# Attention on one Trainium2 core: exponentials turned unnormalised into alternating banks, values per branch in one pass, query tiles in order 3 0 2 1

## The reference

```python
p_c = _masked_softmax(s_c, (cmp_end[None, :] <= t[:, None]))     # compressed keys, 31 of them
o_c = jnp.einsum('bgrqn,bngd->bqgrd', p_c, v_cmp)
...
s_s = s_s - slopes[...] * d_s                                     # keys of the same sequence
p_s = _masked_softmax(s_s, m_s)
o_s = jnp.einsum('bgrqm,bgqmd->bqgrd', p_s, v_sel)
...
p_w = _masked_softmax(s_w, m_w)                                   # window of 512 keys
o_w = jnp.einsum('bgrqk,bkgd->bqgrd', p_w, vwb)
return gate0 * o_c + gate1 * o_s + gate2 * o_w                    # then * silu(z), then @ w_out
```

## Time and profile before

| what | value |
|---|---|
| median of 3 runs | 1343.09 us (1340.88 to 1346.35) |
| the profiled execution, its own time | 1339.4 us |
| its span in the profile | 1337.6 us |
| PE busy | 1275.8 us, 95% |
| DVE, ACT, POOL busy | 788.0 us, 434.3 us, 840.3 us |
| granted clock of PE, mean | 0.991 |
| attention stage, first scores to first matmul of the output product | 852.83 to 1017.81 us |

### The profile page before, as it was taken

How to read it: one execution, slowest core, us unless ns; L and a number is a source line. 1 busy time by engine, 2 the same in 40 slices (tenths; PEclk the granted TensorE clock), 3 DMA queues, 4 the chain that set the end, 5 groups by cost and what they waited for, 6 DMA issues and landing times.

```text
span 1337.6 us, 22823 instructions
## 1 busy us (share of the span) xinstructions
PE 1275.8 (95%) x8112; PEld 1015.6 (76%) x8112; DVE 788.0 (59%) x1214; ACT 434.3 (32%) x866; POOL 840.3 (63%) x1062
## 2 busy tenths in 40 slices
PE   6999998999999999999999999899999999999996
PEld 4778897778877788888788798555557787878884
DVE  5978664589699211598347235378773649832223
ACT  4165744243301133211200021677773200331111
POOL 6767632677999777899678728200003875467872
PEclk9999999899999999999999999999999999999998
DMA  5222100253325433354494213100004469623331
GB/s 194 74 85 79 49 4 16 79 140 94 95 78 198 158 101 94 93 159 150 110 349 133 73 30 95 32 2 1 1 1 160 147 143 265 207 72 97 100 95 71
DMA packets 86478, 137.93 MB, mean 103 GB/s; under 512 B 16512, under 2 KB 34432, under 8 KB 85376
## 3 DMA queue, kind: packets, MB, share of 16 engines
q1 hardware_dynamic: 48384, 88.10, 22.1%
q10 hardware_dynamic: 38016, 48.71, 11.5%
HBM read 119.02 MB, written 20.91 MB: 105 GB/s over the span
## 4 chain that ended last, share of the span: by engine, by line
PE 81%; DVE 8%; issue 4%; POOL 3%; ACT 2%; ACTq 1%; DMA 1%; POOLq 0%; DVEq 0%
PE ps L388 20%; PE ps L389 20%; PE ps L390 20%; PE ps L783 3%; PE ps L794 3%; PE ps L806 3%; PE ps L541 2%; POOL small L1404 2%; DVE acc L1494 1%; PE ps L687 1%; PE ps L732 1%; DVE bigB L1991 1%; PE ps L862 1%; POOL wh L1405 1%; PE ps L531 1%
## 5 line engine op out<-in xcount | busy, mean ns | idle before, releaser
L1407 POOL TENSOR_TENSOR wl<-raw,wh 128x512 fp32r<-128x512 f32 x336 | 500.4, 1489 | 27.0
L1404 POOL TENSOR_TENSOR small<-small 1x1 f32<-1x1 f32 x336 | 122.0, 363 | 304.4 <-PE ps L390 298.2
L388 PE MATMUL ps<-uH,wh 128*128 128x512 f32 x672 | 266.6, 397 | 11.1 <-DVE uL L1484 11.1
L390 PE MATMUL ps<-uH,wl 128*128 128x512 f32 x672 | 263.0, 391 | 0.0
L389 PE MATMUL ps<-uL,wh 128*128 128x512 f32 x672 | 262.7, 391 | 0.0
L1405 POOL CAST wh<-raw 128x512 fp32r<-128x512 f32 x336 | 202.9, 604 | 0.0
L388 PEld LDWEIGHTS ps<-uH,wh 128*128 128x128 f32 x672 | 127.0, 189 | 40.6 <-issue 11.2
L389 PEld LDWEIGHTS ps<-uL,wh 128*128 128x128 f32 x672 | 127.1, 189 | 27.3 <-issue 1.4
L390 PEld LDWEIGHTS ps<-uH,wl 128*128 128x128 f32 x672 | 126.9, 189 | 26.6
L388 PE MATMUL ps<-ffH,wh 128*128 128x512 f32 x256 | 101.3, 396 | 4.4 <-POOL wl L1407 4.3
L389 PE MATMUL ps<-ffL,wh 128*128 128x512 f32 x256 | 99.8, 390 | 0.0
(11 more groups left out here) (387 smaller groups left out, 2428.2 us busy)
## 6 DMA issues: line engine op xcount, KB each, us to landing
raw<-wstream SPq DMA_DIRECT2D x336, 256.0 KB, 2.6
b_powers_scratch<-bigB ACTq DMA_DIRECT2D x4, 1024.0 KB, 4.9
c_powers_scratch<-bigB ACTq DMA_DIRECT2D x8, 512.0 KB, 4.4
lags_scratch<-lag_rows_scratch ACTq DMA_DIRECT2D x8, 512.0 KB, 9.0
bigB<-b_powers_scratch ACTq DMA_DIRECT2D x4, 1024.0 KB, 8.9
bigB<-lags_scratch ACTq DMA_DIRECT2D x4, 1024.0 KB, 5.9
bigB<-c_powers_scratch ACTq DMA_DIRECT2D x4, 1024.0 KB, 9.0
hT<-x ACTq DMA_DIRECT2D x4, 512.0 KB, 7.3
```

What stands on the lines that cost most here:

```text
L388: pe.matmul(out, lh, rh, start=first, stop=False)
L390: return pe.matmul(out, ll, rh, start=False, stop=last)
L1404: pool.tensor_tensor(small[0:1, 569 + j:570 + j], zero_ap[0:1], zero_ap[0:1], ALU.add)
L1407: pool.tensor_tensor(wl[:, j, :], raw[:, j, :], wh[:, j, :].bitcast(f32), ALU.subtract).then_inc(half_split, 1)
```

## The change

- **Units** become (t, b, qt) with qt in the order 3, 0, 2, 1: four units make a *group*, one head pair and one branch; there are 16 groups.
- **`weigh` is gone.** `prob` (six buffers now) is turned as exp leaves it, four units after its scores (`LAG`), where it was two.
- **`turn`** writes query tiles 2 and 3 to banks 4 and 5, and query tiles 0 and 1 to bank 6. ACT still evicts tiles 0, 1 and 2; DVE evicts tile 3 (`tensor_copy`, 128x1024).
- **`probT`** is two buffers of a whole group, in the place of `pcT`. **`values`** runs once per group into bank 7: per key tile kt and half one matmul over the columns from 128 kt to 512.
- **Weights per row.** DVE inverts a group's eight sums at once (`invert`), POOL multiplies them by the gates and spreads the result over 128 x 512 (`spread_gates`), PE turns that in four transposes into bank 6 (`spread`), DVE multiplies it by silu(z) (`weights`) and the values in bank 7 by the product (`finish`), then adds: branch 0 to the compressed branch's part in `mixT`, branch 1 to that.
- **The compressed branch** is done at the head of the stage: `cmp_values` for the eight head pairs, 512 columns wide, into banks 6 and 7 by turns, and `cmp_branch` on DVE, which multiplies by silu(z) into `mixT`.
- Slopes are made on POOL between the groups' products, in the same number.

The lines removed are those of the printed functions; of the diff the core stands here.

```diff
-        prob = view(bigB, 9216, 3, 2, 512)
-        probT = view(bigB, 12288, 3, 2, 512)
+        prob = view(bigB, 9216, 6, 2, 512)
+        probT = [view(bigB, 4096 * i, 2, TT, 512) for i in range(2)]
...
-        asum = small[:, 544:550].rearrange("p (u b) -> p u b", b=2)
-        UNITS = [(t, qt, b) for t in range(KT) for qt in range(TT) for b in range(2)]
+        asum, rsum = (small[:, at:at + 16].rearrange("p (g t a) -> p g t a", g=2, a=2) for at in (576, 592))
+        rz, branch, spread_gates = (bigA[:, 14336 + 512 * i:14848 + 512 * i] for i in range(3))
+        UNITS = [(t, b, qt) for t in range(KT) for b in range(2) for qt in (3, 0, 2, 1)]
+        NGROUP = 2 * KT
+        LAG = 4
...
+        def turned(qt):
+            src = ps[:, 4:6, 0:(qt + 1) * 128] if qt >= 2 else ps[:, 6, 0:(qt + 1) * 256].rearrange("p (a k) -> p a k", a=2)
+            return src.rearrange("p a (k c) -> p a k c", c=128)
...
             def turn(u):
-                pe.wait_ge(at_p, u + 1)
+                t, b, qt = UNITS[u]
+                g = u // 4
+                pe.wait_ge(at_e, u + 1)
+                if qt >= 2:
+                    pe.wait_ge(at_long, u // 2)
+                elif qt == 0:
+                    pe.wait_ge(at_short, 2 * g)
+                    pe.wait_ge(cs_p, TT + KT)
+                else:
+                    pe.wait_ge(at_short, 2 * g + 1)
+                    if g:
+                        pe.wait_ge(at_g, 2 * g - 1)
                 for half in range(2):
                     for kt in range(qt + 1):
+                        at = half * 512 + kt * 128 if qt >= 2 else 1024 + (half * (qt + 1) + kt) * 128
+                        i = pe.transpose(ps[:, 4 + at // 512, at % 512:at % 512 + 128], prob[:, u % 6, half, kt * 128:(kt + 1) * 128], ident)
...
-            def values(u):
...
+            def cmp_values(t):
+                if t >= 2:
+                    pe.wait_ge(cs_p, TT + t - 1)
+                for half in range(2):
+                    g = t // 4 * 2 + half
+                    i = pe.matmul(ps[64 * half:64 * half + 64, 6 + t % 2, :], vcmp[:, g * DH:(g + 1) * DH], pcT[:, half * 8 + t, :],
+                                  start=True, stop=True)
+                i.then_inc(cs_t, 1)
+            def values(g):
+                t, b = g // 2, g % 2
+                pe.wait_ge(at_long, 2 * g + 2)
+                pe.wait_ge(at_short, 2 * g + 2)
+                if g:
+                    pe.wait_ge(at_g, 2 * g)
+                else:
+                    pe.wait_ge(cs_p, TT + KT)
+                for kt in range(TT):
                     for half in range(2):
+                        h = t // 4 * 2 + half
+                        i = pe.matmul(ps[64 * half:64 * half + 64, 7, kt * 128:512], vtok[:, kt, b * 256 + h * DH:b * 256 + (h + 1) * DH],
+                                      probT[g % 2][:, half, kt, kt * 128:512], start=kt == 0, stop=kt == TT - 1)
                 i.then_inc(at_v, 1)
+            def spread(g):
+                pe.wait_ge(at_x, g + 1)
+                pe.wait_ge(at_short, 2 * g + (3 if g < NGROUP - 1 else 2))
+                for qt in range(TT):
+                    i = pe.transpose(ps[:, 6, qt * 128:(qt + 1) * 128], spread_gates[:, qt * 128:(qt + 1) * 128], ident)
+                i.then_inc(at_v, 1)
+            for n in range(4 * NGROUP + LAG + 3):
+                g, first = (n - LAG - 2) // 4 - 1, n >= LAG + 6 and (n - LAG - 2) % 4 == 0
+                if first:
+                    values(g)
                 if n < len(UNITS):
                     scores(n)
-                if 2 <= n <= len(UNITS) + 1:
+                if n < 2:
+                    for t in range(4 * n, 4 * n + 4):
+                        cmp_values(t)
+                if LAG <= n < len(UNITS) + LAG:
+                    turn(n - LAG)
+                if first:
+                    spread(g)
...
+            for n in range(len(UNITS) + LAG):
+                if n >= LAG and UNITS[n - LAG][2] < 3:
+                    u = n - LAG
+                    g, qt = u // 4, UNITS[u][2]
                     act.wait_ge(at_t, u + 1)
+                    if u % 4 == 1:
+                        if g >= 2:
+                            act.wait_ge(at_v, 2 * g - 3)
+                        else:
+                            act.wait_ge(cs_t, 16 + KT)
+                    act.activation(probT[g % 2][:, :, 0:qt + 1, qt * 128:(qt + 1) * 128], turned(qt), ACT.Copy).then_inc(
+                        at_long if qt >= 2 else at_short, 1)
                 if n < len(UNITS):
+                    t, b, qt = UNITS[n]
                     W = (qt + 1) * 128
                     act.wait_ge(at_s, n + 1)
                     for half in range(2):
+                        i = act.activation(prob[:, n % 6, half, 0:W], prob[:, n % 6, half, 0:W], ACT.Exp, scale=-1.0,
+                                           bias=anmax[:, n % 3, half:half + 1], accum_out=asum[:, n // 4 % 2, qt, half:half + 1])
...
-                if n >= 14 and n % 8 == 6:
+                if n >= 12 + LAG and (n - LAG) % 8 == 4:
+                    lead(uH[:, (n - LAG) // 8 - 1, :])
...
+            def slopes(t):
                 if t >= 2:
                     pool.wait_ge(at_s, 8 * (t - 1))
+                for half in range(2):
+                    pool.tensor_scalar(dsl[t % 2][:, half, :], const("dist"), const("slope")[:, half * 8 + t:half * 8 + t + 1], 0.0,
+                                       ALU.mult, ALU.add).then_inc(ds_ready, 1)
+            slopes(0)
+            slopes(1)
+            for g in range(NGROUP):
+                t, b = g // 2, g % 2
+                if b and t + 2 < KT:
+                    slopes(t + 2)
+                pool.wait_ge(cs_sub, TT + g + 1)
+                if g:
+                    pool.wait_ge(at_v, 2 * g)
+                pool.tensor_tensor(spread_gates.rearrange("p (t a d) -> p t a d", a=2, d=DH),
+                                   rsum[:, g % 2].unsqueeze(3).to_broadcast([128, TT, 2, DH]),
+                                   gate[:, :, 1 + b, t::KT].unsqueeze(3).to_broadcast([128, TT, 2, DH]), ALU.mult).then_inc(at_x, 1)
...
                 if u >= 3:
+                    dve.wait_ge(at_e, u - 2)
+                if u >= 6:
+                    dve.wait_ge(at_t, u - 5)
                 for half in range(2):
+                    i = dve.tensor_tensor_reduce(prob[:, u % 6, half, 0:W], ps[:, u % 2 * 2 + half, 0:W],
...
-            def weigh(u):
...
-            def finish(t):
...
+            def cmp_branch(t):
+                dve.wait_ge(cs_t, 16 + t + 1)
+                dve.tensor_tensor(mixT[:, t, :], ps[:, 6 + t % 2, :], zsT[:, t, :], ALU.mult).then_inc(cs_p, 1)
+            def invert(g):
+                dve.wait_ge(at_e, 4 * g + 4)
+                dve.reciprocal(rsum[:, g % 2], asum[:, g % 2]).then_inc(cs_sub, 1)
+            def weights(g):
+                dve.wait_ge(at_v, 2 * g + 2)
+                dve.tensor_tensor(rz, ps[:, 6, :], zsT[:, g // 2, :], ALU.mult).then_inc(at_g, 1)
+            def finish(g):
+                t, b = g // 2, g % 2
+                dve.wait_ge(at_g, 2 * g + 1)
+                dst = branch if b else xs[:, t % 2, :]
+                dve.tensor_tensor(dst, ps[:, 7, :], rz, ALU.mult).then_inc(at_g, 1)
+                dve.wait_ge(at_g, 2 * g + 2)
+                if b:
+                    dve.tensor_tensor(xs[:, t % 2, :], xs[:, t % 2, :], branch, ALU.add).then_inc(x_full, 1)
+                else:
+                    dve.wait_ge(cs_p, TT + KT)
+                    own(dve.tensor_tensor(xs[:, t % 2, :], xs[:, t % 2, :], mixT[:, t, :], ALU.add))
...
+            for n in range(4 * NGROUP + LAG + 4):
                 if n < len(UNITS):
                     shift(n)
-                    weigh(n - 1)
+                if n < 2:
+                    for t in range(4 * n, 4 * n + 4):
+                        cmp_branch(t)
+                if LAG <= n < len(UNITS) + LAG and UNITS[n - LAG][2] == 3:
+                    u = n - LAG
+                    g = u // 4
+                    dve.wait_ge(at_t, u + 1)
+                    if g >= 2:
+                        dve.wait_ge(at_v, 2 * g - 3)
+                    dve.tensor_copy(probT[g % 2][:, :, :, 384:512], turned(3)).then_inc(at_long, 1)
+                if n >= 5 and n % 4 == 1 and n // 4 <= NGROUP:
+                    invert(n // 4 - 1)
+                if n >= LAG + 6 and (n - LAG) % 4 == 2:
+                    weights((n - LAG - 2) // 4 - 1)
+                if n >= LAG + 7 and (n - LAG) % 4 == 3:
+                    finish((n - LAG - 3) // 4 - 1)
+                if n >= LAG + 15 and (n - LAG) % 8 == 7:
+                    finish_rest((n - LAG - 7) // 8 - 1)
```

More of the change, by code:

```diff
@@ L272, in build @@
         ds_ready = sem("slopes_ready")
-        at_qk, at_s, at_e, at_p, at_t, at_ev, at_v, at_o = (sem(f"att_{n}") for n in
-            ("scores", "scores_read", "exp", "probs", "transposed", "probsT", "value", "out"))
```

(32 more changed lines are left out.)

43 lines of the change are left out of this document (2 added, 41 removed).

## The result

The changed kernel takes 1330.34 us in the median of four runs (1328.44 to 1331.12), the kernel before 1342.55; the ratio is 0.9905 with a 95% interval of 0.9887 to 0.9923. The forecast was 9.4 us less, and measured are 12.2, with bounds of about 10 and 15 us. In the profiled pair the stage from the first scores to the output product's first matmul goes from 164.98 to 155.66 us, 9.3 less, where the forecast had 155.6.

What follows compares the result with a forecast made beforehand. PE's queue was taken to bound the stage: sixteen groups 143.0, compressed values 8.2, head and tail 2.6, low clock 1.8, together 155.6 against 165.0 us. Taking 9.4 off 1343.09 gave 1333.7, range 1325 to 1343.

Steps and rivals of the forecast that it cites:

- PE's phases bound the stage, the 0.16 comes with the phase: PE's queue in the stage: each change of phase costs 0.16 us; `values` in one phase takes 2.29 instead of 2.78.
- Column halves pair at 512: In `values`: the two column halves run side by side at 512 columns, 2.29 us per group instead of 4.4.
- The rival with 34 us more: In `values`: column halves don't pair at 512 columns, 34 us more, 1367.8 us; chance 0.04.
- The waits for `weigh` and the collision with POOL: At the last tile's turn: PE waits about 1.0 us per head pair; POOL's slopes add 0.79 in six, 4.7 in all.
- The hand-off over bank 6, 0.3: Before tile 1's turn: PE waits 0.3 us per group for DVE's `weights` to read what `spread` wrote.
- Head and tail, 2.6: PE's waits at the stage's ends: about 1.0 at the head, 1.0 and 0.75 at the tail, 0.1 for first `cmp_values`.
- `spread`, 0.59: Four new PE transposes per group: 0.59 us with a phase gap, 0.43 without; 0.59 was taken.
- the rival that gained more: `spread` has no gap behind the turn (2.6 us) and the hand-off wait is covered (4.8): 1326.3 us; chance 0.06.
- "1.8 (the same low clock)": At the stage's start: the low clock costs 1.8 us, the same as in the kernel before.
- the sum's 15.0: First scores to first turn: 4.0 us of scores, 8.2 of compressed values, 1.0 of waits, 1.8 for the clock.
- "With turning four units late, exp has some 8 us of slack, so the waits go.": At the turns: turning four units after the scores gives exp some 8 us of slack, so waits for `weigh` go.
- DVE, ACT and POOL hidden: In mid stage: DVE at 7.4 of 8.9 us (83%), ACT and POOL's new products cost nothing because PE is longer.

Runs made afterwards that it cites:

- narrow values: The changed kernel with `values` in one phase but 128 columns at a time, 40 records instead of 16: group 8.80 us, stage 157.6 us.
- its own run: The kernel before, without POOL's slopes of head pairs 2 to 7: stage 160.3 us instead of 165.0.
- four edits: The changed kernel turning two, three or five units after the scores, or with tile order 3 1 2 0: groups 9.07, 8.56, 8.49 and 8.98 us.
- lag 3: The changed kernel turning three units after the scores: stage 152.6 us; with compressed values of 128 rows, the added weight rows zero: stage 146.5, median 1321.46 us.
- lag 5: The changed kernel turning five units after the scores: stage 152.6 us; with compressed values of 128 rows, the added weight rows zero: stage 146.8, median 1321.66 us.

## Why the prediction was right

The time, 1330.34, lies in the range of 1325 to 1343 and 3.4 under the forecast of 1333.7; the stage's sum of 155.6 was met by 155.66, but by terms that were off and cancelled, and that is luck. The groups are 2.7 us shorter than forecast, the rest of the head and the tail 1.2, and the low clock costs 5.8 where 1.8 was put down, 4.0 more.

- *PE's phases bound the stage, the 0.16 comes with the phase.* Right. `values` 2.30 for 2.29, and the narrow values show that the phases count and not the matmuls.
- *Column halves pair at 512.* Right: 2.38 for 16 records. The rival with 34 us more is out.
- *The waits for `weigh` and the collision with POOL.* Right, 4.7 us for the collision by its own run, and about 13.7 for the waits as a whole, where the terms of the prediction (4.7, and 1.0 for each head pair) give some 13.
- *The hand-off over bank 6, 0.3.* Right, 0.32 in its place, and four edits moved it as the chain says.
- *Head and tail, 2.6.* The waits at the tail were right: 0.95 before the last turn and 0.77 before the last values, for 1.0 and 0.75. The terms as told add up to 2.85; they give 2.6 only if the 0.3 that the last group already holds is taken off, which the prediction doesn't say.
- *`spread`, 0.59.* Mis-sized: the lower bound was the true value, 0.43: turn and `spread` together take 1.24, and 0.80 of that is the turn. That is 16 x 0.15 = 2.4 us less, most of the 16 x 0.17 = 2.7 by which the groups are shorter than forecast. It is half of the rival that gained more; its other half, the hand-off, came true only under other lags.
- *"1.8 (the same low clock)".* The step that failed. I carried the loss of the kernel before over to a head with other work in it: the wide compressed values with 31 rows, priced at full clock. The loss was 6.7 us, and the run with 128 rows puts what it cost the stage at 5.8. The head came out 3.3 us longer to the first turn than the sum's 15.0 (at full clock it is 12.6, a little under the 13.2 of the sum).
- *"With turning four units late, exp has some 8 us of slack, so the waits go."* The waits went, but the reason is too broad: with two units they go as well.
- *DVE, ACT and POOL hidden.* Right. `weights` beside POOL's product keeps 0.69, and PE never waits for the eviction of tile 3 in mid stage. DVE's price for that eviction was 1.2 and is 1.21; DVE is busy 15.42 of 20 us, 77%, where 83% was forecast.

## What to carry to other kernels

When an in-order queue bounds a stage, write it down as phases from start to start, then ask of each hand-over between engines how long the round is and how long the work standing between is: here five kernels with the same work differ by 0.6 us a group through that alone. Work taken off another engine pays only by the wait it caused on the bounding one, and part of that wait may be a collision with a third engine, here 4.7 of some 13.7 us. Moved work doesn't take the old clock with it: look at the granted clock in the stretch that it goes to, and at what the engine does there.

## What was not expected of the hardware

Matmuls with 31 rows and 512 columns, one behind the other with PE busy throughout, ran at a granted clock of 0.50, the level of 1.2 GHz, from 855 to 865 us; the same matmuls with 128 rows, same columns and same count, ran at 1.00, and sixteen records took 3.81 us instead of 7.09. How many rows are enough was not tested. In mid stage of the kernel before, 31-row matmuls in small numbers between others of 128 and 64 rows left the clock at 1.00. Filling the weights' rows with zeros, which costs one memset, made the stage 6.1 us shorter with lag 3 (146.5 for 152.6) and 5.8 with lag 5.

Also, transposes that follow transposes start without the 0.16 us that lies between phases of different shape, across a semaphore wait and with other operands.
